# Experts: hidden rows turned by VectorE block transposes, down weights in consecutive rows, and loads in another order

## The reference

```
proj = x @ w_in                       # 256x1024 @ 1024x4112; the last 16 columns feed the gates
...
u = x @ w_in                          # S5 input, 256x1024 @ 1024x1024
...
logits = xt @ w_router + b_router     # top 2 of 8 experts, softmax over the two
for e in range(8):                    # D_FF_EXPERT = 1408
    y = y + dense_gate[:, e:e + 1] * ((silu(xt @ w1[e]) * (xt @ w3[e])) @ w2[e])
```

## Time and profile before

| | us |
|---|---|
| Median of three runs | 1445.45 |
| Lowest and highest run | 1435.64, 1450.67 |
| Profiled execution | 1451.63 |
| Its span, first to last instruction | 1449.8 |
| PE busy | 1347.9 (93%) |
| VectorE, ScalarE, GpSimd busy | 366.1, 243.6, 181.9 |

### The profile page before, as it was taken

One profiled execution on the slowest core, in us unless ns is written; L12 is line 12 of the kernel. 1 busy time (PEld: TensorE's weight loads), 2 busy tenths in 40 slices (PEclk: granted clock), 3 DMA queues, 4 the chain that ended last, 5 costly groups with the idle time before them and its releaser, 6 DMA issues.

```text
span 1449.8 us, 23908 instructions
## 1 busy us (share of the span) xinstructions
PE 1347.9 (93%) x10525; PEld 895.2 (62%) x10525; DVE 366.1 (25%) x796; ACT 243.6 (17%) x548; POOL 181.9 (13%) x137
## 2 busy tenths in 40 slices
PE   6998999999999979997999999888848989999997
PEld 5887996877777747445544554344326646776673
DVE  0635644251253064224000000000022152000001
ACT  2342232121010102411110111011011021000000
POOL 1020000407567000000200000000334000000000
PEclk9999999999999989997999999999978989999999
DMA  9424010796433762837999999999989240433520
GB/s 319 151 82 145 2 59 0 211 373 227 154 111 120 94 175 41 329 133 268 388 326 339 395 345 325 370 360 328 356 254 329 75 163 1 156 134 116 199 91 29
DMA packets 111116, 292.65 MB, mean 202 GB/s; under 512 B 6412, under 2 KB 41328, under 8 KB 111056
## 3 DMA queue, kind: packets, MB, share of 16 engines
q1 hardware_dynamic: 98128, 259.93, 53.4%
q0 software_dynamic: 4944, 15.19, 3.6%
q10 hardware_dynamic: 7984, 16.65, 3.5%
HBM read 274.58 MB, written 17.17 MB: 201 GB/s over the span
## 4 chain that ended last, share of the span: by engine, by line
PE 75%; SPq 11%; DMA 6%; DVE 4%; ACT 2%; issue 2%; POOL 0%; ACTq 0%; DVEq 0%; POOLq 0%
PE bank L1551 23%; PE bank L2030 8%; PE bank L2173 8%; PE bank L1564 6%; PE bank L2056 5%; PE bank L1850 4%; PE bank L1978 4%; DMA arena<-moe_w 3%; PE bank L1528 3%; SPq L537 3%; PE bank L1557 2%; SPq L528 2%; PE bank L1904 2%; SPq L534 2%; SPq L529 2%
## 5 line engine op out<-in xcount | busy, mean ns | idle before, releaser
L1551 PE MATMUL bank<-xT,arena 128*128 128x256 f32 x1696 | 378.5, 383 | 5.1 <-DMA arena<-gdn_w_in 2.3
L1551 PEld LDWEIGHTS bank<-xT,arena 128*128 128x128 f32 x1696 | 323.1, 192 | 56.8 <-issue 8.1
L2030 PE MATMUL bank<-arena 128*32 128x352 f32 x3072 | 233.6, 462 | 18.6 <-DMA arena<-moe_w 17.6
L2030 PEld LDWEIGHTS bank<-arena 128*32 128x32 f32 x3072 | 101.5, 110 | 148.4 <-issue 113.4
L2056 PE MATMUL bank<-arena 128*32 128x256 f32 x2112 | 116.4, 380 | 3.0 <-DMA arena<-moe_w 3.0
L2173 PE MATMUL bank<-arena 128*128 128x512 f32 x256 | 111.0, 592 | 0.0
L2056 PEld LDWEIGHTS bank<-arena 128*32 128x32 f32 x2112 | 67.4, 110 | 49.5 <-DMA arena<-moe_w 4.9
L2173 PEld LDWEIGHTS bank<-arena 128*128 128x128 f32 x256 | 48.6, 190 | 58.2 <-issue 57.9
L1528 PE MATMUL bank<-const,arena 128*128 128x128 f32 (+1 forms) x432 | 57.3, 276 | 29.2 <-DVE arena L1154 22.4
L1138 DVE TENSOR_TENSOR arena<-arena,bank 128x352 f32<-128x352 f32 x24 | 12.5, 522 | 241.8 <-PE bank L2030 241.8
L1528 PEld LDWEIGHTS bank<-const,arena 128*128 128x128 f32 (+1 forms) x432 | 47.7, 143 | 40.1 <-DVE arena L1154 22.8
(11 more groups left out here) (345 smaller groups left out, 1272.5 us busy)
## 6 DMA issues: line engine op xcount, KB each, us to landing
arena<-moe_w SPq DMA_DIRECT2D x64, 1408.0 KB, 24.3
arena<-ffn_w SPq DMA_DIRECT2D x33, 1024.0 KB, 10.2
arena<-moe_w SPq DMA_DIRECT2D x32, 1024.0 KB, 20.3
arena<-gdn_w_in SPq DMA_DIRECT2D x8, 2048.0 KB, 9.9
arena<-w_up SPq DMA_DIRECT2D x8, 2048.0 KB, 8.3
arena<-w_down SPq DMA_DIRECT2D x8, 2048.0 KB, 7.7
slot_rows<-arena ACTq DMA_DIRECT2D x1, 9600.0 KB
arena<-moe_w SPq DMA_DIRECT2D x24, 384.0 KB, 20.9
```

Source lines behind the costliest of these rows:

```text
L1551: last = mm(bank[:, at:at + SEQ], w[:, k, P * m:P * m + P], x[:, k, :], start=(k == 0), stop=(k == KT - 1))
L2030: last = mm(banks[i][32 * q:32 * q + 32, 0:EW1], xg[:, EK * s + kk, 32 * t:32 * t + 32], w[:, kk, EW1 * q:EW1 * q + EW1], start=(s == 0 an ...
```

## The change

Five things are changed.

1. The product of silu and up is written in another order of channels: channel 11 f + x of a quarter goes to column 32 x + f. VectorE then transposes 32x32 blocks of the whole row (`mhT[:, t]`), so that partition p holds the eleven inner channels 11p to 11p+10. PE's nine transposes, ScalarE's 15 copies per expert and the semaphore between them are gone.
2. The down weights are loaded to match: partition p takes eleven consecutive rows, three to a slab (two to the last), in one transfer per slab.
3. In the beginning the identity alone is loaded ahead of x, the input slabs follow with no wait, the other constants after the first slab; the gate product stands after four tiles; GpSimd's gate weights wait for x, its layer-norm vectors for eight tiles.
4. The S5 input weights are loaded ahead of the tables, and the last tables wait for the earlier ones too.
5. The clearing of `mh` is gone; the last fetch waits for a signal of ScalarE instead of doing a dummy add.

```diff
-        mh = region(38688, ST, 3 * P)
-        mhT = region(39840, FE_T, ST, 32)
+        mh = region(38688, ST, EW1)
+        mhT = region(39840, ST, EW1)
...
-            sp.dma_start(const[:], A["shape_const"].rearrange("p (a b) -> p a b", b=P)).then_inc(const_loaded, 16)
+            ident_in = A["shape_const"].rearrange("p (a b) -> p a b", b=P)
+            sp.dma_start(const[:, 0:1], ident_in[:, 0:1]).then_inc(x_loaded, 16)
             sp.dma_start(xres[:], A["x"][0].rearrange("(n p) d -> p n d", p=P)).then_inc(x_loaded, 16)
...
-            sp.wait_ge(vecs_loaded, 48)
-            sp.wait_ge(ba_w_loaded, 16)
             for b in range(8):
...
+                if b == 0:
+                    sp.dma_start(const[:, 1:N_CONST], ident_in[:, 1:N_CONST]).then_inc(const_loaded, 16)
...
+            sp.wait_ge(up_done, 2 * FC * FF_CHUNKS)
+            for c in range(2):
+                load(sp, ("s5_in", c), 7 + c, s5_in_w[c], rows(A["s5_w_in"][0], 4 * c, 4))
             sp.wait_ge(kz_stored, 64)
             sp.wait_ge(xrow_loaded, 16)
-            sp.wait_ge(up_done, 2 * FC * (FF_CHUNKS - 2))
             sp.wait_ge(down_done, FF_CHUNKS - 2)
             for j in range(NPIECE - 1):
                 table_loads(j)
-            sp.wait_ge(up_done, 2 * FC * FF_CHUNKS)
-            for c in range(2):
-                load(sp, ("s5_in", c), 7 + c, s5_in_w[c], rows(A["s5_w_in"][0], 4 * c, 4))
+            sp.wait_ge(t_loaded, 32 * SUB * (NPIECE - 1))
             sp.wait_ge(u_done, 4)
             table_loads(NPIECE - 1)
...
-                w2e = A["moe_w2"][0][bass.ds(e, 1)]
+                w2e = A["moe_w2"][0][bass.ds(e, 1)].rearrange("e (p x) d -> p (e x) d", p=P)
...
-                    w2q = w2e[:, EW1 * q:EW1 * q + EW1].rearrange("e f d -> (e f) d")
-                    sp.dma_start(m2[q][:, 0:2], w2q[0:2 * P].rearrange("(b p) d -> p b d", p=P)).then_inc(m_loaded[EC + q], 16)
-                    if q < EC - 1:
-                        f0 = EW1 * EC - ER + 32 * q
-                        sp.dma_start(m2[q][0:ER, 2], w2q[2 * P:EW1]).then_inc(m_loaded[EC + q], 16)
-                        sp.dma_start(m2[q][ER:P, 2], w2e[:, f0:f0 + 32].rearrange("e f d -> (e f) d")).then_inc(m_loaded[EC + q], 16)
+                    sp.dma_start(m2[q][:, 0:min(3, FE_T - 3 * q)], w2e[:, 3 * q:min(3 * q + 3, FE_T)]).then_inc(m_loaded[EC + q], 16)
...
+            pool.wait_ge(x_loaded, 32)
             pool.dma_start(region(38984, KT, 16), A["gdn_w_in"][0].rearrange("(k p) f -> p k f", p=P)[:, :, 4096:4112]).then_inc(ba_w_loaded, 16)
...
+            nc.gpsimd.memset(pre[:, :, 0:CONV - 1], 0.0).then_inc(pad_ready, 1)
+
+            pool.wait_ge(in_tile, 8)
             norm_load(0, "ln_g", 0)
             norm_load(1, "ln_b", 0)
-            nc.gpsimd.memset(pre[:, :, 0:CONV - 1], 0.0).then_inc(pad_ready, 1)
-
+            pool.wait_ge(const_loaded, 16)
...
-            pool.wait_ge(m_y, n_pass * (EXPERTS * (EC + 2)))
-            pool.wait_ge(y_stored, n_pass * (64 * EXPERTS) + 64)
-            link(nc.gpsimd.tensor_tensor(pool_pad, zero_c, zero_c, ALU.add))
+            pool.wait_ge(routed, 4)
...
-            link(V_.memset(mh, 0.0))
...
-                    V_.tensor_tensor(mh[:, t, 0:EW1], msil[:, t], banks[2 * t + 1][:, 0:EW1], ALU.mult).then_inc(m_h, 1)
+                    V_.tensor_tensor(mh[:, t].rearrange("p (x f) -> p f x", x=FE_T), msil[:, t].rearrange("p (f x) -> p f x", x=FE_T),
+                                     banks[2 * t + 1][:, 0:EW1].rearrange("p (f x) -> p f x", x=FE_T), ALU.mult).then_inc(m_h, 1)
+                    dve.wait_ge(m_h, k * ST + t + 1)
+                    V_.transpose(mhT[:, t], mh[:, t]).then_inc(m_hT, 1)
...
-                for t in range(ST):
-                    take_hT(t)
...
+            act.wait_ge(y_stored, n_pass * (64 * EXPERTS) + 64)
+            act.sem_inc(routed, 1)
...
-            pe.wait_ge(const_loaded, 16)
+            pe.wait_ge(x_loaded, 32)
             pe.wait_ge(vecs_loaded, 48)
...
             for m in range(24):
+                if m == 4:
+                    pe.wait_ge(const_loaded, 16)
+                    gate_product()
...
-                pe.wait_ge(t_loaded, 16 * 2 * SUB * (j + 1))
+                pe.wait_ge(t_loaded, 32 * SUB * max(j + 1, NPIECE - 1))
...
-                pe.wait_ge(m_h, k * ST + 2)
-                hidden(0)
-                hidden(1)
+                pe.wait_ge(m_hT, k * ST + 1)
...
-                pe.wait_ge(m_h, k * ST + 3)
-                hidden(2)
...
-                        for b, m in ((0, c), (1, EC + c), (2, 2 * EC + c)):
-                            if m == FE_T:
-                                continue
+                        for x in range(3 * c, min(3 * c + 3, FE_T)):
                             for q in range(EC):
-                                last = mm(y_bank[t][32 * q:32 * q + 32, 0:EW2], mhT[:, m, t], m2[c][:, b, EW2 * q:EW2 * q + EW2],
+                                last = mm(y_bank[t][32 * q:32 * q + 32, 0:EW2], mhT[:, t, 32 * x:32 * x + 32], m2[c][:, x % 3, EW2 * q:EW2 * q + EW2],
```

More of the change, by code:

```diff
@@ L1260, in _, with gates @@
             take_x(1)
-            act.wait_ge(ba_v, 1)
-            link(A_(tmp_b, tmp_a, ACT.Abs, bias=zero_c))
-            link(A_(tmp_b, tmp_b, ACT.Exp, bias=zero_c, scale=-1.0))
-            A_(a_log, a_log, ACT.Exp, bias=zero_c).then_inc(ba_a, 1)
-            A_(tmp_b, tmp_b, ACT.Ln, bias=one_c).then_inc(ba_a, 1)
-            link(A_(beta, ba[:, :, 0:8], ACT.Sigmoid, bias=zero_c))
+            def gates():
+                act.wait_ge(ba_v, 1)
+                link(A_(tmp_b, tmp_a, ACT.Abs, bias=zero_c))
+                link(A_(tmp_b, tmp_b, ACT.Exp, bias=zero_c, scale=-1.0))
+                A_(a_log, a_log, ACT.Exp, bias=zero_c).then_inc(ba_a, 1)
+                A_(tmp_b, tmp_b, ACT.Ln, bias=one_c).then_inc(ba_a, 1)
+                link(A_(beta, ba[:, :, 0:8], ACT.Sigmoid, bias=zero_c))
             def decays():
@@ L1304, in _ @@
                         A_(root, banks[5][:, 0:256].rearrange("p (n a b) -> p n a b", n=NT, b=8)[:, :, :, 0], ACT.Sqrt, bias=eps_rms).then_inc(root_ready, 1)
-                if b:
+                if b == 0:
+                    gates()
+                else:
                     take_silu(b - 1)
@@ L1459, in _ @@
                 act.dma_start(xrow, slots[bass.ds(k + 1, 1)].rearrange("a s d -> (a s) d")).then_inc(xrow_loaded, 16)
-                def take_hT(t):
-                    act.wait_ge(m_tr, k * ST + t + 1)
-                    nc.scalar.copy(mhT[:, 0:2 * EC, t], banks[2 + t][:, 0:2 * P].rearrange("p (m i) -> p m i", i=32))
-                    nc.scalar.copy(mhT[0:ER, 2 * EC:FE_T, t], banks[2 + t][0:ER, 2 * P:3 * P - 32].rearrange("p (m i) -> p m i", i=32))
-                    for j in range(3):
-                        last = nc.scalar.copy(mhT[ER:P, 2 * EC + j, t], banks[2 + t][32 * j:32 * j + 32, 3 * P - 32:3 * P])
-                    last.then_inc(m_hT, 1)
                 for t in range(ST):
@@ L1574, in _, with gate_product @@
             need_x()
-            w_ba = region(38984, KT, 16)
-            pe.wait_ge(ba_w_loaded, 16)
-            for n in range(NT):
-                last = token_major(banks[6 + n][:, 0:16], xT, w_ba, n)
-            last.then_inc(ba_done, 1)
+            def gate_product():
+                w_ba = region(38984, KT, 16)
+                pe.wait_ge(ba_w_loaded, 16)
+                for n in range(NT):
+                    last = token_major(banks[6 + n][:, 0:16], xT, w_ba, n)
+                last.then_inc(ba_done, 1)
             def cumulated_g():
@@ L2013, in _ @@
             with pe.Fori(0, n_pass * EXPERTS) as k:
-                def hidden(t):
-                    for b in range(3):
-                        last = transpose(four(banks[2 + t])[:, b], mh[:, t, P * b:P * b + P])
-                    last.then_inc(m_tr, 1)
                 pe.wait_ge(xg_ready, k * 2 + 2)
@@ L2043, in _ @@
                     last.then_inc(gath_done, 1)
[L2044 to L2045 removed]
                 y_bank = (banks[6], banks[7], banks[4])
                 for c in range(EC):
[L2048 removed]
+                    pe.wait_ge(m_loaded[EC + c], (k + 1) * 16)
                     for t in range(ST):
```

6 lines of the change are left out of this document (2 added, 4 removed).

## The result

The changed kernel took 1397.7 us, median of 4 runs (1396.07 to 1398.98); the kernel before took 1441.37 beside it (4 runs, 1435.64 to 1450.67). The ratio is 0.969, with a 95% interval of 0.963 to 0.975: faster, by 3.1%. The forecast was 1401, between 1390 and 1418. The profiled execution took 1396.07 us, its span 1394.2, against 1451.63 and 1449.8 before: 55.6 us of span went. Ratios leave out the few runs of the kernel before that were over 1.5% above its fastest, so they can differ a little from the ratio of the medians given.

What follows compares the result with a forecast made beforehand. PE bounds the kernel, except where it waits for weights. Experts 33.5, beginning 4.6, S5 input 10.6 and small edits 0.5 sum to 49.2 us off 1451.63, so 1402.4, taken as 1401; range 1390 to 1418.

Steps and rivals of the forecast that it cites:

- Experts, down weights: Expert stage: w2 in whole transfers goes from 260 to 414 GB/s, so PE sets the pace; stage with turn −33.5 us.
- Rival (a): Experts: w2 stays at 260 GB/s and DMA still ends them, 1436; partial cures under 320 GB/s, 1412 to 1436; chance 0.09.
- rival (c): Each expert's w2 stretch: contiguous 12 KB runs are slower than the old pieces; 1482 at 200 GB/s, 1505 at 180; chance 0.05.
- The lead of 29 us: Experts: loaded weights run near 29 us ahead of PE, from four experts without a wait while DMA fell back 7.4 each.
- Experts, the turn: Between up and down products: nine PE transposes go, 0.95 us per expert, to 43.63; VectorE's new work is charged nothing.
- I keep 0.52 for the product: VectorE's product of silu and up, written at a stride of 32 elements, still takes 0.52 us per tile.
- the upper bound of 8 us: At slowest VectorE rates, three tiles released 1.18 us apart queue there; PE waits 1.0 us per expert, 8 in all.
- rival (b): Experts: VectorE late with the third hidden tile, down products wait, 8 us at most, 1409; chance 0.06.
- Beginning: Start of the kernel: earlier input slabs and a moved gate product end the eighth tile at 45.2, before 49.77: −4.6 us.
- The fall of the clock behind the moved gate product: Beginning: the moved product may pull PE's clock down in dense work, costing 3.4 us; given a half, not in the sum.
- S5 input: S5 input product: weights issued ahead of the tables end PE's waits; end 549.1 instead of 559.92, counted −10.6 us.
- Small edits: Clearing of the hidden tile gone: 0; dummy GpSimd add before the last row fetch gone: −0.5 us, between 0 and −0.8.

Runs made afterwards that it cites:

- the kernels at 283 and 290: Changed kernel, third block of down-weight slabs 0 to 2 loaded to 96 and 32 partitions (283 GB/s): 1434.13 us; or two halves of 64 (290): 1433.78 us.
- Its own experiment: Changed kernel with the beginning as before (constants ahead of x, gate product ahead of the tiles): 1395.76 us, beside 1392.83 of the changed kernel.
- the plain product: Changed kernel with VectorE's product of silu and up written in order, without the stride of 32 elements: 1393.51 us, ratio 0.962.

## Why the prediction was right, and where its steps were off

*Experts, down weights: right.* 33.7 us came of 33.5 forecast. w2 arrives at the pace of other whole tiles, in rows of 12 KB or 4, in one transfer or two; the pieces alone, put back, bring the waits back. Rival (a) and rival (c) are refuted by the windows of 402 to 422 GB/s, which also hold against the Trainium skill's limit of about 358 GB/s for loads from HBM (DMA: Bandwidth & Descriptors, "Where 436 GB/s comes from"): the trace does not agree with it here. That section gets the 358 by dividing an HBM stack's bandwidth between two cores, and here one core ran alone; what two would get no run shows. The lead of 29 us was sized well: with the pieces back, the first wait is in the fourth expert. The threshold for rival (a), 320 GB/s for w2, fits the runs but was not met closely by any: the kernels at 283 and 290 waited, that with two whole transfers at 415 did not.

*Experts, the turn: the sum right, two terms and one bound wrong.* PE's pace is 43.59, forecast 43.63. The step "I keep 0.52 for the product" failed: it takes 0.80, the price of the reordered form. The transpose, taken at 0.52, takes 0.546. Together 1.35 against 1.04 per tile; 0.66 us of cover was left instead of 0.9. And "the three tiles, released 1.18 us apart, queue on VectorE" was wrong: 2.37 apart, since the last slab has two groups of products for each tile, for silu and for up. So the upper bound of 8 us and rival (b) rested on a queue that can't form at these durations, nor at the bound's own 1.7 us per tile. The run with a second transpose, for which I had still believed in it, showed that.

*Beginning: right, the clock overrated.* 5.4 came against 4.6. PE started its tiles at 12.89 and not at 13.70. The fall of the clock behind the moved gate product had been given a half; it came in one of eleven profiled executions with the moved product. It cost 3.3 us there (eighth tile ended at 47.7, against 44.3 to 44.6 in the four others that started quickly), as priced (3.4). What I had not seen is another slow start. In six of the eleven the first products went at half the pace until about 17 us, and the eighth tile ended at 46.2 to 46.9. The first of the next two windows is of the changed kernel in the group above, the second of the one that the result is of:

```profile
13.00:17.00 4.00, 3.95 (x9) 3.16 (x10) 0.00 (x0) 0.00 (x0) 0.00 (x0) 1.00 1.00 327
```

```profile
13.00:17.00 4.00, 4.00 (x19) 3.54 (x20) 0.00 (x0) 0.32 (x1) 0.00 (x0) 1.00 1.01 344
```

Nine products against nineteen. The column of the clock says 1.00 in both, but the record of the clock begins only at 17.3 us in the first and at 11.9 in the second, so the pace tells here and the column doesn't. The beginning is therefore worth 3 to 5.4 us. Its own experiment could not show that in the total, for the reason given there.

*S5 input: right.* 10.4 against 10.6 (the prediction's own ends, 559.92 and 549.1, are 10.8 apart; it counted 10.6): 7.6 in the product (35.80 from its first start to its end, now 28.17) and 2.7 in its earlier start. The clock stood at 1.00 throughout, as taken (28.17 for all 512 products, forecast 27.8). Putting the old order back cost 9.8 to 10.1 at the place and 9.6 in the median, so nearly all of it is the order.

*Small edits: one not contradicted, one too large.* The clearing of `mh` has no run of its own, and no gain that could be its own shows. The fetch edit is worth 0.23 in place of 0.5, inside its bounds of 0 to 0.8.

*What the sum did not have.* The last store lands 3.5 us sooner, since there is hardly other traffic when DMA is no longer late: I had asked who waits for weights, and not what else is pushed back with them. The 2.4 us between the S5 input and the experts are mostly the clock's and not the change's. The clock fell there for 6.8 and 20.5 us in the kernel before and for 3.4 and 17.1 in the changed one, and three kernels with all or most of the change whose clock fell for 6.8 and 20.5 as well (the beginning as it was, the plain product, the second transpose) take 123.3 to 123.5 for this stage, against 123.8 before and 121.4 in the changed kernel; three others whose clock fell as in the changed kernel take 121.5. So about 0.4 is left that could be the change's. The span lost 55.6 where the sum had 49.2. The forecast lies only 3.3 above the median all the same: of the 6.4 that the sum lacked, 1.4 had been taken off for the level of the runs, and the median lies 1.6 above the profiled execution. That closeness is in part luck, for another pair of executions would give other stages: by the medians the change is worth 43.7, less than the sum. The reason given for the 1.4, that the runs spread in the experts as long as DMA bounds them, was not shown: the two kernels with slow pieces spread over 11 to 12 us in ten runs each, but the changed kernel, in the group where it ran again, over 15 in four.

## What to carry to other kernels

When an expert or a layer falls back to DMA's pace, cut the stretch by what is in flight and compare GB/s, not the share of busy DMA engines: transfers to a part of the partitions held this queue at 265 to 290 GB/s while the share read 1.03. Shape weight slabs so that every transfer goes to all 128 partitions, if need be by renumbering channels; the length of a partition's run did not matter between 4 and 12 KB here. Compare more than one pair of executions before a small difference between stages is put down to an edit. To judge new work on a side engine, take from the timeline how far apart its inputs are released and when its result is wanted, before a bound is multiplied by the number of tiles.

## What the runs showed of the hardware that I had not expected

- Two transfers to 64 partitions each, one behind the other in the queue, are nearly as slow as 96 and 32: a slab takes 6.0 and 6.6 us, 4.0 with a whole transfer in their place. The whole transfers of the same slabs are slowed too (425 and 452 ns for a packet of 8192 B, 324 otherwise), and those around them land in 25.0 us for 1408 KB in place of 12.9.
- An element-wise product of 352 f32 per partition with its operands read and written in a reordered form (the result at a stride of 32 elements) takes 800 ns, 521 in plain order. A copy of 64 elements at such a stride had shown nothing of it.
- VectorE's block transpose of 128x352 f32 takes 546 ns, about what a plain product of that size does.
- The clock's falls are no fixed property of a stretch. Near 90 us it fell in most profiled executions, those of the kernel before among them, for up to 3.3 us, but not in three of the fourteen, with the same instructions there. In the last part of the kernel there is likewise a difference of 3.9 us between executions of the changed kernel (357.0 and 353.1); the longer one has a fall of 6.8 us at 1131 us that the shorter one lacks, and a longer one at 1019 (23.9 us against 20.5).
- A small store, in a queue of its own, took 5.30 us to land while another queue loaded weights at 379 GB/s, and 1.8 when next to nothing else was moved (14 GB/s).
